# Loads reordered, latent splits moved, modulation's halves added on GpSimd, one eviction moved, in a two-block fp32 transformer kernel

## What is computed

```python
def hybrid_layer(x, c, pos, ...):
    mod = (silu(c) @ w_ada + b_ada)[:, None, :]
    shift_a, scale_a, gate_a, shift_f, scale_f, gate_f = split(mod, 6)
    h = rms_norm(x, attn_norm) * (1.0 + scale_a) + shift_a
    (nq, nkc, nvc, nks, nvs, nkw, nvw, ngate, cq, ckv, kr, bgate) = split(h @ w_in)
    kc = rms_norm(compress(rope(nkc), cmp_k_pe, cmp_k_w1, cmp_k_w2), nsa_kc_norm)
    vc = compress(nvc, cmp_v_pe, cmp_v_w1, cmp_v_w2)
    o_a = nsa_mixer(q_a, kc, vc, ks, nvs, kw, nvw, sigmoid(ngate))
    q_b = rms_norm(cq, mla_cq_norm) @ w_uq
    kv_b = rms_norm(ckv, mla_ckv_norm) @ w_ukv
    o_b = mla_mixer(q_b, k_b, v_b)      # after norms and rope
    x = x + gate_a * ((g_a * o_a + g_b * o_b) @ w_o)
    h = rms_norm(x, ffn_norm) * (1.0 + scale_f) + shift_f
    x = x + gate_f * ((silu(gt) * val) @ w_down)   # of conv(h @ w_up)
    return x

def second_block(h, ...):
    for layer in range(2):
        m = mixer(rms_norm_2(h, norm_mix_pre[layer]))   # shortconv_fox, then conformer
        h = h + rms_norm_2(m, norm_mix_post[layer])
        f = swiglu_ffn(rms_norm_2(h, norm_ffn_pre[layer]), ...)
        h = h + rms_norm_2(f, norm_ffn_post[layer])
```

## Time and profile before

| | |
|---|---|
| median of 3 runs | 1191.25 us (1190.74 to 1191.29) |
| profiled execution: its own time | 1185.71 us |
| its span in the trace | 1184.4 us |
| mean granted TensorE clock | 0.977 |
| busy: PE / DVE / ACT / POOL | 1135.3 / 750.6 / 591.0 / 31.2 us |
| DMA | 207.81 MB, mean 175 GB/s |

### The profile page before, as it was taken

How to read it: one execution, slowest core, us unless ns; L and a number is a source line. 1 busy time by engine, 2 the same in 40 slices (tenths; PEclk the granted TensorE clock), 3 DMA queues, 4 the chain that set the end, 5 groups by cost and what they waited for, 6 DMA issues and landing times.

```text
span 1184.4 us, 19309 instructions
## 1 busy us (share of the span) xinstructions
PE 1135.3 (96%) x7814; PEld 1029.4 (87%) x7814; DVE 750.6 (63%) x1411; ACT 591.0 (50%) x1043; POOL 31.2 (3%) x32
## 2 busy tenths in 40 slices
PE   8999799999899999998998999999999999999998
PEld 7988688888679999888987799998878978999986
DVE  3576576787667788765656666665455556666644
ACT  3464274444556666435334564444365356444532
POOL 0350000000000000001000000000000000000000
PEclk9999899899899999999989999999999999999999
DMA  8945654454135555563623185554544314655450
GB/s 344 387 169 203 234 206 178 150 206 154 38 130 196 182 187 190 210 231 139 234 104 107 56 285 182 179 190 168 177 174 160 107 72 151 197 189 190 131 193 35
DMA packets 30796, 207.81 MB, mean 175 GB/s; under 512 B 3539, under 2 KB 4051, under 8 KB 7156
## 3 DMA queue, kind: packets, MB, share of 16 engines
q1 hardware_dynamic: 30708, 206.58, 48.8%
HBM read 205.52 MB, written 1.05 MB: 174 GB/s over the span
## 4 chain that ended last, share of the span: by engine, by line
PE 85%; DVE 7%; ACT 4%; issue 2%; DMA 2%; SPq 0%; ACTq 0%; DVEq 0%
PE ps L392 47%; PE ps L1634 19%; PE ps L622 3%; PE ps L410 2%; DVE wlo L351 2%; DMA raw<-uq 1%; ACT whi L344 1%; PE ps L2235 1%; PE ps L2267 1%; DVE tm L565 1%; PE ps L1333 1%; PE ps L1759 1%; PE ps L1411 1%; PE ps L581 1%; PE ps L1136 1%
## 5 line engine op out<-in xcount | busy, mean ns | idle before, releaser
L351 DVE TENSOR_TENSOR wlo<-raw,whi 128x1024 fp32r<-128x1024 f32 (+2 forms) x328 | 371.1, 1173 | 254.5 <-ACT whi L344 254.2
L392 PE MATMUL ps<-H_h,whi 128*128 128x256 f32 x1552 | 447.0, 288 | 2.5 <-DVE wlo L351 2.5
L392 PE MATMUL ps<-H_l,whi 128*128 128x256 f32 x1552 | 440.9, 284 | 0.0
L392 PE MATMUL ps<-H_h,wlo 128*128 128x256 f32 x1552 | 440.9, 284 | 0.0
L344 ACT ACTIVATE whi<-raw 128x1024 fp32r<-128x1024 f32 (+2 forms) x328 | 315.5, 1011 | 187.3 <-PE ps L1634 113.0
L392 PEld LDWEIGHTS ps<-H_h,whi 128*128 128x128 f32 x1552 | 299.0, 193 | 6.9 <-issue 6.6
L392 PEld LDWEIGHTS ps<-H_l,whi 128*128 128x128 f32 x1552 | 298.7, 192 | 0.7 <-issue 0.5
L392 PEld LDWEIGHTS ps<-H_h,wlo 128*128 128x128 f32 x1552 | 298.4, 192 | 0.0
L1634 PE MATMUL ps<-whi,gl_h 128*128 128x512 f32 x264 | 105.6, 400 | 0.5 <-DVE wlo L351 0.5
L1634 PE MATMUL ps<-whi,gl_l 128*128 128x512 f32 x264 | 104.6, 396 | 0.0
L1634 PE MATMUL ps<-wlo,gl_h 128*128 128x512 f32 x264 | 104.6, 396 | 0.0
(11 more groups left out here) (445 smaller groups left out, 1532.7 us busy)
## 6 DMA issues: line engine op xcount, KB each, us to landing
raw<-f SPq DMA_DIRECT2D x44, 1024.0 KB, 4.9
raw<-win SPq DMA_DIRECT2D x27, 1024.0 KB, 6.9
raw<-ada SPq DMA_DIRECT2D x24, 1024.0 KB, 6.0
raw<-up SPq DMA_DIRECT2D x22, 1024.0 KB, 4.9
raw<-g SPq DMA_DIRECT2D x20, 1024.0 KB, 4.9
raw<-pw SPq DMA_DIRECT2D x12, 1024.0 KB, 4.9
raw<-down SPq DMA_DIRECT2D x10, 1024.0 KB, 4.9
raw<-wa SPq DMA_DIRECT2D x4, 1024.0 KB, 9.9
```

What stands on the lines that cost most here:

```text
L351: dve.tensor_tensor(wlo[j % NS][:, a:b], raw_of(key)[:, a:b], whi[j % NS][:, a:b].bitcast(F32), ALU.subtract).then_inc(w_lo.hit(key, half), 1)
L392: ins_ = pe.matmul(bank[:, m * 256:(m + 1) * 256], wt[a][:, kt * w + col + m * 128:kt * w + col + m * 128 + 128], act[b][:, k0 + kt, :], s ...
```

## The change

1. **Order of loads** (`_order`): `wg` comes before `cv1`/0; all three units of `uq` come earlier, `cv1`/1 to 3 and `ada`/9 and 10 later. The order in which units are split stays the same.
2. **Latent stage.** On DVE the low part of `uq`/1 is made right behind modulation 8's products, ahead of gates and rope; behind these come `uq`/2's, `kcn`, modulation 8's result, `ukv`/0's low part, and only then modulation 9's products. On PE the gates' transposes move behind `uq`/1 and the sum of 9 behind `ukv`/0.
3. **Halves added on GpSimd.** A new function `ada_pool` adds the second accumulator onto the first (128 x 256 fp32, 16 times: units 8 to 10 in the latent stage, 11 to 19 in the attention, 20 to 23 in the down projection). PE waits for that (`ada_both`) and does one matmul in the wide form, two in the narrow one.
4. **Mixer's start.** The eviction of `win2`/6 moves behind the low part of `win2`/8.

```diff
--- before.py
+++ after.py
@@ -71,9 +71,9 @@
     for i in (2, 3):
         seq("wa", i, i + 1), seq("wb", i, i + 1)
     seq("win", 0, 1), seq("win", 4, 6), seq("ck1", 0, 1), seq("win", 6, 7), seq("ck1", 1, 2), seq("win", 1, 2)
-    seq("ck1", 2, 3), seq("win", 2, 3), seq("ck1", 3, 4), seq("win", 3, 4), seq("cv1", 0, 1), seq("wg"), seq("ada", 8, 9)
-    seq("cv1", 1, 2), seq("uq", 0, 1), seq("cv1", 2, 3), seq("uq", 1, 2), seq("cv1", 3, 4), seq("ada", 9, 10), seq("uq", 2)
-    seq("ukv", 0, 1), seq("ada", 10, 11), seq("ukv", 1)
+    seq("ck1", 2, 3), seq("win", 2, 3), seq("ck1", 3, 4), seq("win", 3, 4), seq("wg"), seq("cv1", 0, 1), seq("uq", 0, 1)
+    seq("ada", 8, 9), seq("uq", 1, 2), seq("cv1", 1, 2), seq("uq", 2), seq("cv1", 2, 4), seq("ukv", 0, 1), seq("ada", 9, 11)
+    seq("ukv", 1)
     seq("win", 7, 10), seq("ada", 11, 13), seq("win", 10, 11), seq("ada", 13, 14), seq("win", 11, 12)
     seq("ada", 14, 16), seq("win", 12, 13), seq("ada", 16, 17), seq("win", 13, 14), seq("ada", 17, 19)
     seq("win", 14, 15), seq("ada", 19, 20), seq("wo")
@@ -269,6 +269,7 @@
     w_hi, w_lo, unit = sig("w_hi"), sig("w_lo"), sig("unit")
     const_set, c_exp, c_silu = sig("const_set"), sig("c_exp"), sig("c_silu")
     ada_sum, ada_row, ada_col, mod_set = sig("ada_sum"), sig("ada_row"), sig("ada_col"), sig("mod_set")
+    ada_both = sig("ada_both")
     sq_set, stat, rs_ln, rs = sig("sq_set"), sig("stat"), sig("rs_ln"), sig("rs")
     n_mul, n_hi, n_lo = sig("n_mul"), sig("n_hi"), sig("n_lo")
     zeroed, tab_set = sig("zeroed"), sig("tab_set")
@@ -574,17 +575,21 @@
         if old:
             pe.wait_ge(*old)
         where["col", u] = b
-        pe.wait_ge(*ada_sum(u, 7))
-        x = asum(u)
+        pe.wait_ge(*ada_both(u))
+        x = asum(u)[0]
         if u in BC_OF:
-            for j in range(2):
-                ins_ = pe.matmul(b[:, 0:256], ones[:], x[j], start=j == 0, stop=j == 1)
-            ins_.then_inc(ada_col.hit(u), 1)
+            pe.matmul(b[:, 0:256], ones[:], x, start=True, stop=True).then_inc(ada_col.hit(u), 1)
             return
         for m in range(2):
-            for j in range(2):
-                ins_ = pe.matmul(b[:, m:m + 1], x[j][:, m * 128:m * 128 + 128], ones[:, 0:1], start=j == 0, stop=j == 1)
+            ins_ = pe.matmul(b[:, m:m + 1], x[:, m * 128:m * 128 + 128], ones[:, 0:1], start=True, stop=True)
         ins_.then_inc(ada_col.hit(u), 1)
+
+    def ada_pool(pool, us):
+
+        for u in us:
+            x = asum(u)
+            pool.wait_ge(*ada_sum(u, 7))
+            pool.tensor_tensor(x[0], x[0], x[1], ALU.add).then_inc(ada_both.hit(u), 1)
 
     def mod_dve(dve, u):
         dve.wait_ge(*ada_col(u))
@@ -1083,7 +1088,7 @@
                 where["uq", i, half] = b
                 mm_fm(pe, ("uq", i), cqn, normed("vs") if (i, half) == (0, 0) else held, b, half * 256,
                       done=unit.hit("uq", i) if half else half_done.hit("uq", i))
-            if i == 0:
+            if i == 1:
                 b, old = M.take(gt_set(2))
                 if old:
                     pe.wait_ge(*old)
@@ -1091,12 +1096,12 @@
                 pe.wait_ge(*gt_set(1))
                 pe.transpose(b[:, 0:24], grow[:, 0:128], cc("ident")[0:24, 0:24])
                 pe.transpose(b[:, 24:48], grow[:, 128:256], cc("ident")[0:24, 0:24]).then_inc(gt_turn.hit(), 1)
+            if i == 0:
                 key_norm_pe(pe)
                 ada_sums_pe(pe, 8)
             if i < 2:
                 cmp_pe(pe, "cv", 2 + i)
         hidden_pe(pe, 1)
-        ada_sums_pe(pe, 9)
         for half in range(4):
             b, old = G.take(ev_act("ukv", 0, half))
             if old:
@@ -1114,6 +1119,7 @@
             pe.matmul(pm[:, 0:256], cc("perm32"), mqr[:, half, :], start=True, stop=True).then_inc(
                 perm_done.hit("mq", half), 1)
             mla_stat_pe(pe, "mq", half, where["sqr", half][:, 0:256], ("ones_lo", "ones_hi"))
+        ada_sums_pe(pe, 9)
         for half in range(4):
             b, old = G.take(ev_act("ukv", 1, half))
             if old:
@@ -1200,6 +1206,7 @@
     def latent_dve(dve):
         next_lo(dve, ("wg", 0))
         ada_dve(dve, 8)
+        next_lo(dve, ("uq", 0))
         dve.wait_ge(*gt_exp())
         dve.tensor_scalar(grow[:], grow[:], 1.0, None, ALU.add).then_inc(gt_set.hit(0), 1)
         dve.wait_ge(*gt_set(0))
@@ -1208,15 +1215,13 @@
         dve.wait_ge(*ev_act("ck", 2))
         rope_dve(dve, "kr", CK[:, 5:6, :], where["pm", "kr"][:, 0:256].unsqueeze(1), tabs["mk"][0][:], tabs["mk"][1][:],
                  krb[:].unsqueeze(1), 1)
-        for i in range(3):
-            next_lo(dve, ("uq", i))
-            if i == 1:
-                key_norm_dve(dve)
-                mod_dve(dve, 8)
-                ada_dve(dve, 9)
+        next_lo(dve, ("uq", 1))
+        key_norm_dve(dve)
+        mod_dve(dve, 8)
+        next_lo(dve, ("uq", 2))
+        ada_dve(dve, 9)
         dve.wait_ge(*gt_turn())
         dve.tensor_copy(gt[:], where["gt"][:, 0:48].rearrange("p (t g) -> p t g", g=24)).then_inc(gt_set.hit(2), 1)
-        mod_dve(dve, 9)
         next_lo(dve, ("ukv", 0))
         hidden_dve(dve, 1)
         for half in range(4):
@@ -1226,6 +1231,7 @@
             if half == 2:
                 value_dve(dve)
         next_lo(dve, ("ukv", 1))
+        mod_dve(dve, 9)
         ada_dve(dve, 10)
         for half in range(4):
             if half:
@@ -1271,6 +1277,7 @@
     def latent_pool(pool):
         table_pool(pool, "mq", "mq_rope", "mq_rsw", "cosr", "sinr")
         table_pool(pool, "mk", "mk_rope", "mk_rsw", "cosr", "sinr")
+        ada_pool(pool, range(8, 11))
 
 
     class Job:
@@ -1577,6 +1584,7 @@
         pool.wait_ge(*m_rope("mk", 3))
         for i in range(2):
             pool.memset(ptc[i], 0.0).then_inc(zeroed.hit("ptc", i), 1)
+        ada_pool(pool, range(11, 20))
 
 
     STATS = {n: 8 * i for i, n in enumerate(("F", "mix0", "m_wout2", "ffn0", "m_g0", "mix1", "m_pw2", "ffn1", "m_g1"))}
@@ -1983,10 +1991,16 @@
     def fox_dve(dve, i):
         key = ("win2", i)
         next_lo(dve, key)
+        if i == 7:
+            dve.wait_ge(*rn_set("mix0"))
+            fox_out_dve(dve, 6)
+        if i != 6:
+            fox_out_dve(dve, i)
+
+    def fox_out_dve(dve, i):
+        key = ("win2", i)
         dve.wait_ge(*unit(*key))
         z, k = v2(where[key][:]), 2 * (i % 2)
-        if i == 6:
-            dve.wait_ge(*rn_set("mix0"))
         if i < 2:
             dve.tensor_tensor(gbt[:, k:k + 2, :], z, bc2(rn[:]), ALU.mult).then_inc(ev_dve.hit("gb", i), 1)
         elif i < 4:
@@ -2175,6 +2189,7 @@
         jobs_dve(dve, FOX, soft_f, fill, lambda h: mask_dve(dve, h), done)
 
     def mix0_pool(pool):
+        ada_pool(pool, range(20, 24))
         pool.wait_ge(*unit("down", 11))
         pool.memset(fk[:], 0.0).then_inc(zeroed.hit("fk"), 1)
         pool.memset(fv[:], 0.0).then_inc(zeroed.hit("fv"), 1)
```

## The result

The changed kernel takes **1174.65 us** (median of 4, 1172.25 to 1175.00) against 1191.27; the ratio is 0.985, 95% interval 0.9828 to 0.9873. The direction was right, the forecast size was half of what came.

The account below looks back on a forecast made before the run. The prediction took TensorE (PE), busy 96% of 1184.4 us, as the bound. Terms of -4.9 (latent stage), -2.5 (mixer), -1.7 (down projection) and +1.5 (attention) gave -7.6 us: 1183.6, range 1178.5 to 1187.5.

Parts of the forecast that it names:

- term of -3.9 for the stall: Latent stage: `uq`/2 issued earlier, so PE's wait for `kcn` shrinks from 7.6 us to about 4 and PE restarts at 135.5.
- rival A: Clock stays up through the shorter gap, another 1.9 us, or additions cost 0.71 us, another 1.2: 1180.5 us; chance 0.15.
- B: Latent stage: PE waits before `uq`/0 for a late `cv1`/1 landing, losing part of the 4.9: 1186.5 to 1188; chance 0.08.
- C: Only part of the `kcn` stall goes, -2 for -4.9 (1186.5), or additions take 1.7 us (1187.8); chance 0.13.
- the clock's return: Latent stage, kernel before: clock at half until about 143.3, 3.9 us after PE's restart; the same again costs +0.5 us.
- -0.44 for `ukv`'s landing: Latent stage: ScalarE's 0.44 us wait for `ukv`/1 goes, since `cv1`/2 frees its place around 138.
- term of +1.5: Attention: additions on GpSimd lengthen the close sums, net +1.5 us, bounds +0.3 to +5.7.
- GpSimd's operation: Attention: one addition taken at 0.95 us, the median of the nearest row, whose shortest was 0.71 and longest 1.70.
- rival D: Attention: additions shut out by VectorE set the pace and the clock falls; slower, 1193.5 to 1195 us; chance 0.04.
- additions longer than 2 us: GpSimd: a sign that would make the forecast wrong; sixteen additions between 0.7 and 1.7 us were expected.
- Down projection and mixer's start: Four sums lose 0.43 us each, -1.7; PE's wait for a low part at the mixer's start goes, -2.5.
- The difference carried over: The 5.5 us between profiled execution and median was kept, turning 1178.1 for a profiled run into 1183.6 for the median.

Follow-up runs that it names:

- e8_attn_pe: The changed kernel with the nine sums of the attention back on PE, two matmuls each in place of an addition on GpSimd and one: 1176.82 us, ratio 0.9878.
- c1_after: The changed kernel, unchanged, looked at again in more executions: 1174.57 us, ratio 0.9869 to the kernel before, six runs from 1173.21 to 1179.52.
- e3_sums: The kernel before with only part 3, the additions on GpSimd: 1188.05 us, ratio 0.9978.
- e10_no_prog: The changed kernel without part 2, with VectorE's and PE's latent programs as before: 1177.25 us, ratio 0.9885.
- b4_best: The changed kernel with `kcn` ahead of `uq`/2's low part, `cv1`/2 ahead of modulation 8's sum, the attention's sums back on PE, second run: 1171.09 us, ratio 0.9828.
- e5_no_sums: The changed kernel without part 3, all sums with both matmuls on PE: 1183.72 us, ratio 0.9936; ten runs from 1176.04 to 1185.35.

## Why the prediction was right or wrong

The start of the same matmul in the kernel before (its usual execution, the repeated one) and in the changed kernel's first profile, from PE's timelines:

| place | before, us | changed, us | difference | step from the row above | forecast |
|---|---|---|---|---|---|
| `uq`/0 begins | 128.10 | 128.38 | +0.3 | | |
| sum of modulation 8 | 143.34 | 137.05 | -6.3 | -6.6 | -3.9 |
| first compressed scores | 188.59 | 182.22 | -6.4 | -0.1 | -1.0 |
| last values of the attention | 317.41 | 311.87 | -5.5 | +0.8 | +1.5 |
| end of down projection | 545.52 | 538.33 | -7.2 | -1.7 | -1.7 |
| behind the mixer's start | 563.01 | 553.08 | -9.9 | -2.7 | -2.5 |
| mixer's attention begins | 598.45 | 588.52 | -9.9 | 0.0 | 0 |
| behind its small matmuls | 608.59 | 594.33 | -14.3 | -4.3 | 0 |
| end | 1189.7 | 1173.7 | -16.0 | -1.7 | 0 |

**The steps that failed.** Between these two executions the changed kernel is 16.0 us shorter; the forecast's terms are 7.6. The term of -3.9 for the stall was mis-sized and measured -6.6, 2.7 us more. And the sum put at nothing what the stretches of half clock that nobody edited would do: -4.3 in the mixer's attention and -1.7 near the end. The others partly cancel (-0.1 for -1.0, +0.8 for +1.5).

**Latent stage: mechanism right, size taken from one execution.** The -3.9 was counted from a restart at 139.40, behind a landing of 8.23 us. The changed kernel's restart is where the forecast put it (137.05 in an execution that was 1.7 us later at `uq`/0 than the first profile, so 135.35 against 135.5), since it no longer hangs on the landing. But the kernel before usually stands for 10.1 us, not 7.6. A stall that ends with a transfer has the transfer's spread; the change took out that spread with the stall. The clock fell in the 4 us gap of both profiles of the changed kernel, as forecast; so that half of rival A did not happen, nor B (no wait for `cv1`/1) or C. But the forecast read the clock's return too early: a mean of 0.67 from 143 to 144 is half clock until 143.7, not 143.3, so 4.3 us after the restart, and in the changed kernel it lasted 5.3 us, until 142.4.

The row behind it gave 0.1 us where 1.0 was forecast. The -0.44 for `ukv`'s landing stood on the first profile alone: in the repeated one ScalarE does not wait for `ukv`, and PE's wait for the square is half as long:

```profile
PE ps L1136 <- ACT sq L1145: 0.5, 1, 0.5
```

The gates' transposes, some 0.2 us, have also moved behind the restart. The rest is not taken apart.

**Attention: the term of +1.5 is not confirmed, not even in sign.** The +0.8 of the table is one pair of executions. The same stretch of PE in the second profile of the changed kernel:

```profile
182.28 3.64 PE L1500 MATMUL ps<-kcn,q 128*128 128x15 f32 x32
...
310.65 0.63 PE L1419 MATMUL ps<-zt,mv 128*128 128x128 f32 x2
```

That start is 128.37 us behind the other, 1.3 less than the first profile's 129.65 (311.87 - 182.22); the kernel before has 128.82, repeated, and 129.24 in its first profile. So the difference lies between -0.9 and +0.8. The two profiles of one kernel differ in their stretches of half clock, as from 268 to 273 us, first and second profile:

```profile
268.00:273.00 5.00, 5.00 (x24) 4.24 (x24) 4.65 (x22) 2.03 (x7) 0.00 (x0) 0.66 0.43 182
```

```profile
268.00:273.00 5.00, 5.00 (x40) 4.74 (x40) 3.75 (x19) 2.82 (x11) 0.00 (x0) 1.00 0.31 131
```

One part of the term was mis-sized for sure, GpSimd's operation: 0.73 to 0.78 us in all nine sums here, where 0.95 was taken; that half of rival A came true. The close sums look like this (unit 14; GpSimd, then PE; start, us, engine, line; before: the earlier trace rows):

```profile
239.21 0.77 POOL L592 TENSOR_TENSOR tm<-tm,tm 128x256 f32<-128x256 f32 x1 [8.44 <-DVE tm L566]
```

```profile
240.12 0.58 PE L584 MATMUL ps<-ones,tm 128*128 128x1 f32 x4 [0.75 <-POOL tm L592]
```

PE starts 0.14 us behind the addition, and what it does itself falls from 1.02 us to 0.58, the 0.43 of the sum. The mechanism of rival D, the shut-out, exists: beside VectorE's low parts the same addition takes 1.70 to 2.92 us. GpSimd and VectorE in the latent stage:

```profile
153.66 2.92 POOL L592 TENSOR_TENSOR tm<-tm,tm 128x256 f32<-128x256 f32 x1 [23.17 <-DVE tm L566]
```

```profile
153.61 2.35 DVE L352 TENSOR_TENSOR wlo<-raw,whi 128x1024 fp32r<-128x1024 f32 x2
```

It ends 0.62 us behind VectorE's two operations, at 156.58, about its own length. The first addition in the down projection does the same (487.07, 2.78 us, beside a low part from 486.91). VectorE pays too: beside the first addition in the latent stage the low part of `uq`/1 takes 2.37 us, where the earlier trace rows have 1.83 for the same shape. GpSimd and VectorE there:

```profile
128.78 1.70 POOL L592 TENSOR_TENSOR tm<-tm,tm 128x256 f32<-128x256 f32 x1 [41.80 <-DVE tm L566]
```

```profile
128.66 2.37 DVE L352 TENSOR_TENSOR wlo<-raw,whi 128x1024 fp32r<-128x1024 f32 x2
```

All this agrees with the Trainium skill, "SBUF — State Buffer", section "SBUF: two separate sides": a VectorE operation with two SBUF inputs and a GpSimd operation hold the shared ports for a whole instruction each. The additions of the earlier trace rows had shown 1.70 us at most, and the forecast called additions longer than 2 us a sign that it is wrong; there are two. But in the attention all nine kept to 0.73 to 0.78, and PE waits for no addition outside it, so the price was paid where nobody waited.

**Down projection and mixer's start: right**, -1.7 and -2.7 for -1.7 and -2.5.

**The carry-over to the median failed.** "The difference carried over" assumed that the profiled execution and the median differ by a constant. They differed by a landing (2.5 us) and by the clock: its shortfall is 27.2 us of the first profile's span, (1 - 0.977) x 1184.4, against 30.9 of the repeated one. In the changed kernel's it is 22.3, and this profile is no lucky one: it is the longest of its four runs. These sums are no lost time as they stand, since the clock is also down where PE waits, as in the gap of the earlier trace rows.

**The stretches of half clock that nobody edited were taken as given.** 4.3 us came from the mixer's attention and 1.7 from a stretch near 950 us that was shorter. That was not forecast and is not the work of part 1, 3 or 4 alone or of parts 1 and 2, whose profiles all have the stretch. It seems to hold in most executions of the changed kernel, not in all: eight of ten have a mean clock of 0.981 or more, and the two at 0.978 took 1178.2 and 1179.5 us. The mean clock is no sure sign of this one stretch, though (`e8_attn_pe` has it at 0.981), and only two of the ten have a profile. Why the clock stays up there is open.

## What to carry to other kernels

A profile is one execution: where a stall ends with a transfer, or the clock is below full speed, look at a second and a third before a stall's size, or the difference to the median, is taken from it. A change that takes a transfer off the path gains the transfer's spread too. Judge a change of a few us here by stage, by PE's start of the same matmul in both traces, since stretches of half clock elsewhere move the total by as much as the change; but take more than one trace of each kernel, since the attention of one and the same kernel differed by 1.3 us. And an operation given to GpSimd should be timed beside what VectorE does there, since the same addition took 0.73 us in one place and 2.92 in another.

## What the runs showed of the hardware that was not expected

The granted clock also fell while PE was busy throughout. Behind the 32 small matmuls of the compressed scores, in the changed kernel's first profile,

```profile
L1500 PE MATMUL ps<-kcn,q 128*128 128x15 f32 x32 | 3.6, 259 | 0.0
```

it goes to 0.50, the 1.2 GHz level, at 186 to 191 us, with no wait of PE in or behind them; the kernel before does the same at 188 to 192. It does not always come: in four of the seventeen profiles (`c1_after`, `e3_sums`, `e10_no_prog`, `b4_best`) the clock stays up there. Another such place is the mixer's attention. And the same program differs by up to 9 us between executions (`e5_no_sums`, 1176.04 to 1185.35) in step with its mean clock (0.982 to 0.975).
